# Two transformer blocks on one core: the second block without its dummy TensorE products

## The reference

```python
for layer in range(2):
    mix = hybrid_mixer(x, ...)              # 16 + 12 heads of attention: latent, top-64 of keys, dilated
    z = layer_norm(ALPHA * x + mix, ...)
    x = layer_norm(ALPHA * z + hier_moe(z, ...), ...)

def hier_moe(t, ...):                       # 4 groups of 8 experts, hidden width 256
    lg = t @ rg_w + rg_b                    # one group of four for each token
    le = (t @ re_w + re_b)[chosen group]    # two experts of its eight
    gate = softmax weights of both, times the group's share
    y = sum over experts e of  ((silu(t @ w_gate[e]) * (t @ w_up[e])) * gate[e]) @ w_down[e]
```

## Time and profile before

| what | value |
|---|---|
| median of three runs | 1687.85 us |
| profiled execution | 1691.36 us |
| its span, first to last instruction | 1689.6 us |
| TensorE busy | 1661.9 us, 98% |
| VectorE, ScalarE busy | 858.1, 652.7 us |
| mean granted TensorE clock | 0.993 |
| read from memory | 394.10 MB |

### The profile page before, as it was taken

How to read it: one execution, slowest core, us unless ns; L and a number is a source line. 1 busy time by engine, 2 the same in 40 slices (tenths; PEclk the granted TensorE clock), 3 DMA queues, 4 the chain that set the end, 5 groups by cost and what they waited for, 6 DMA issues and landing times. The chain is left out here.

```text
span 1689.6 us, 23664 instructions
## 1 busy us (share of the span) xinstructions
PE 1661.9 (98%) x9485; PEld 1262.9 (75%) x9485; DVE 858.1 (51%) x1418; ACT 652.7 (39%) x920; POOL 172.9 (10%) x242
## 2 busy tenths in 40 slices
PE   9999999999999999999999999999999999999996
PEld 7888889999788887999988876444548887544453
DVE  6566564444746656444457855322126885532223
ACT  5456443433445544433344542111115464211111
POOL 2020001111102000111111130000002131000000
PEclk9999999999999999999999999999999999999999
DMA  8544545553654454555366428999995634999995
GB/s 321 186 134 148 174 155 195 180 193 109 240 179 145 150 175 150 196 178 196 102 222 190 151 90 316 409 424 423 424 386 173 185 101 148 334 425 422 423 423 214
DMA packets 156285, 396.64 MB, mean 235 GB/s; under 512 B 20496, under 2 KB 85008, under 8 KB 135696
## 3 DMA queue, kind: packets, MB, share of 16 engines
q1 hardware_dynamic: 156176, 395.18, 64.3%
HBM read 394.10 MB, written 1.05 MB: 234 GB/s over the span
## 5 line engine op out<-in xcount | busy, mean ns | idle before, releaser
L918 PE MATMUL ps<-split,split 128*128 128x256 f32 (+3 forms) x1872 | 631.3, 337 | 1.2 <-DVE split L911 0.7
L922 PE MATMUL ps<-split,split 128*128 128x256 f32 (+3 forms) x1872 | 627.7, 335 | 0.2
L919 PE MATMUL ps<-split,split 128*128 128x256 f32 (+3 forms) x1872 | 623.5, 333 | 0.0
L896 DVE TENSOR_TENSOR split<-ring,split 128x2048 fp32r<-128x2048 f32 x136 | 312.6, 2305 | 253.9 <-ACT split L889 253.8
L918 PEld LDWEIGHTS ps<-split,split 128*128 128x128 f32 x1872 | 351.5, 188 | 36.7 <-issue 2.1
L922 PEld LDWEIGHTS ps<-split,split 128*128 128x128 f32 x1872 | 351.7, 188 | 35.9 <-DVE split L2293 1.3
L919 PEld LDWEIGHTS ps<-split,split 128*128 128x128 f32 x1872 | 352.9, 188 | 33.0 <-issue 0.5
L889 ACT ACTIVATE split<-ring 128x2048 fp32r<-128x2048 f32 x136 | 260.3, 1915 | 278.0 <-PE ps L922 268.9
L1775 PE MATMUL ps<-ring,arena 128*64 128x512 f32 x512 | 112.8, 592 | 0.0
L2943 DVE SCALAR_TENSOR_TENSOR arena<-arena,ps 128x256 f32<-128x256 f32 x32 | 15.4, 481 | 167.1 <-ACT arena L2218 131.6
L1775 PE MATMUL ps<-arena 128*64 128x512 f32 x256 | 98.8, 592 | 0.0
(11 more groups left out here) (262 smaller groups left out, 1781.9 us busy)
## 6 DMA issues: line engine op xcount, KB each, us to landing
ring<-in_w_in SPq DMA_DIRECT2D x52, 1024.0 KB, 5.1
ring<-in_w_gate_up SPq DMA_DIRECT2D x44, 1024.0 KB, 5.3
ring<-in_expert_w_down SPq DMA_DIRECT2D x32, 1024.0 KB, 11.6
ring<-in_expert_w_gate SPq DMA_DIRECT2D x24, 1024.0 KB, 11.5
ring<-in_expert_w_up SPq DMA_DIRECT2D x24, 1024.0 KB, 13.5
ring<-in_w_down SPq DMA_DIRECT2D x22, 1024.0 KB, 4.9
ring<-in_w_in SPq DMA_DIRECT2D x28, 768.0 KB, 4.6
high<-in_expert_w_down SPq DMA_DIRECT2D x16, 1024.0 KB, 11.5
```

The costliest lines, as they stand in the source:

```text
L896: nc.vector.tensor_tensor(split(slot), slot, split(high[:, n % HIGH, :]), ALU.subtract).then_inc(low_done.sem, 1)
L918: nc.tensor.matmul(acc, sh, mh, start=start, stop=False)
L919: nc.tensor.matmul(acc, *second, start=False, stop=False)
L922: return nc.tensor.matmul(acc, *third, start=False, stop=stop)
```

## The change

The calls of `keep_running` in the loop of the second block are taken out, all six. In one execution with one pass in each layer these are 32 dummy products in each layer (16 ahead of `turn_z`; 8 and 4 behind the router, with a wait between them; 4 ahead of the gathers), 22 behind the experts of the first layer, and 5 between the two halves of the second layer's `turn_stream`: 91 in all. The waits stay where they are. The calls in the first block and the 26 products at the start of the second stay too.

```diff
--- before.py
+++ after.py
@@ -1484,8 +1484,6 @@
                         mm = nc.tensor.transpose(acc[:, half * SEQ + t * P:half * SEQ + (t + 1) * P], a, ident[:])
                         if t == TT - 1 and half == 1:
                             fill(mm, ("xT", b))
-                    if t == 0 and l > 0:
-                        keep_running(bank2(("A", 1)), 5)
 
             def turn_z(l):
 
@@ -1694,7 +1692,6 @@
                 pair_out(7, l)
                 output_unit(2, l, js=(1,))
                 output_unit(3, l)
-                keep_running(bank2(("xT2", 3)), 16)
                 turn_z(l)
                 acc = bank2(("router", 0))
                 for n, k in enumerate((0, 2, 1, 3, 4, 6, 5, 7)):
@@ -1705,9 +1702,7 @@
                                               start=(n == 0 and t == 0), stop=(n == KT - 1 and t == TT - 1))
                 fill(mm, ("router", 0))
 
-                keep_running(bank2(("ranks", 0)), 8)
                 pe.wait_ge(hot_done.sem, hot_done.at(l, 1))
-                keep_running(bank2(("ranks", 0)), 4)
                 pe.wait_ge(chosen_done.sem, chosen_done.at(l, 1))
                 acc = bank2(("ranks", 0))
                 of_tile = chosen_flat.rearrange("p (t n) -> p t n", t=TT)
@@ -1820,7 +1815,6 @@
 
                     first = pass_ == 0
                     if first:
-                        keep_running(bank2(("sc", 0, 3)), 4)
                         pe.wait_ge(split_low.sem, split_low.at(l, TT))
                     else:
                         wait_apart(pe, sc_added.sem, sc_added.at(lp - 1, 4))
@@ -1882,8 +1876,6 @@
 
                     with pe.If(passes <= done):
                         skip_pass(PASSES - done)
-                        if l < LAYERS - 1:
-                            keep_running(bank2(("yg", 0, 0, 0)), 22)
                     with pe.Else():
                         moe_pass(done)
                         if done + 1 < PASSES:
```

## The result

The change made the kernel slower: 1699.43 us as the median of five runs (1696.51 to 1702.97), against 1686.42 us before (five runs, 1686.04 to 1688.36). The ratio is 1.0066 with a 95% interval of 1.0055 to 1.0077, so +9 to +13 us with +11.1 in the middle; the medians alone differ by 13.0. The forecast was 1706 us, its range 1693 to 1715. The profiled execution took 1696.51 us, its span 1694.7 us.

The account below looks back on a forecast made before the run. It took TensorE's granted clock as decisive, with late expert starts not given back. Two layers of 3.1 - 0.8 + 4.9 make 14.4, plus 3.5 between layers: +17.9 us on the 1687.85 median, 1706 us, range 1693 to 1715.

Parts of the forecast that it names:

- A: 16 dummies out ahead of the turns: clock falls 3.56 us earlier, turns and router slow, +3.1 us a layer.
- B: 12 dummies out ahead of the ranks: start 1.7 us sooner, products at half clock +0.9; -0.8 us a layer.
- C: 4 dummies out ahead of the gathers: gathers and some gate and up products at half clock, +4.9 us a layer.
- early return: Rival: the gathers themselves bring the clock back, C only 2.6 us; 1700 us in all; chance 0.17.
- D: 27 dummies out between the layers: clock falls in 7.3 idle us, second turns and projection slow, +3.5 us once.
- Only columns slow: Rival: half clock costs a product its columns only, gathers start each 0.160 us; 1693 us; chance 0.06.
- Late return: Rival: gate and up products do not restore the clock, only the second gathers do; C 12.4, 1721 us; chance 0.07.
- faster: Rival: clock falls and returns as before, only the rank dummies' delay goes, -3.5 us; 1684.4 us; chance 0.04.

Follow-up runs that it names:

- e10: Kernel before with each second-block dummy of 512 columns replaced by one f32 product of 36 columns, the router's form: 1702.75 us against 1686.99, ratio 1.0100.
- b1: The kernel before, unchanged, profiled once more: 1688.2 us in one run.
- e7: Kernel before without the dummies ahead of turns, ranks and gathers; the 22 and 5 between the layers stay: 1699.77 us, ratio 1.0067.
- e9: Changed kernel with four dummies added in each layer's router, one behind every fourth product: 1699.68 us, ratio 1.0062 to the kernel before.
- e2: Kernel before without only the 16 dummies ahead of the turns in each layer: 1691.22 us, ratio 1.0025.
- e4: Kernel before without only the 22 dummies behind the experts and the 5 between the turns: 1688.46 us, ratio 1.0002.
- a1: The changed kernel, all six calls out, run once more for another profile: 1698.88 us, ratio 1.0061 to the kernel before.
- e3: Kernel before without only the 4 dummies ahead of the gathers in each layer: 1690.10 us, ratio 1.0015.

## Why the prediction was right, and which steps were not

The mechanism was right: what the dummies do for the second block is to keep the clock or to bring it back, and without them the same products run at half of it. e10 is the proof that idleness as such is not the cause: there TensorE never stops in these layers, and the clock is lost. Over the 93 runs of the changed kernel, b1 and the experiments (mean clock and span of each, half-clock time as twice what the clock lacks of 1 times the span) the time grows by 0.30 us for each microsecond at half clock, with a correlation of 0.95. The slope is rough, since the mean clock is given to 0.001, which is 3.4 us at half clock; and time at half clock in which TensorE waits or issues dummies off the path costs nothing. The size, +18 us, was about half as much again as the +11 to +13 measured. Step by step:

- **A, the turns.** Forecast +3.1 us a layer, by letting the fall come earlier by as much as the dummies had lasted. In four layers of the changed kernel it fell in the router as before twice (8.9 and 8.8 us after the last projection product, before 8.7), and about 3 us after it twice, once coming back in the turns and once not. The last router product starts 9.6, 10.6, 9.6 and 13.7 us after the last projection product, against 9.7 before: +1.2 us in the mean. The prediction took one course for the only one; e7 and e9 show it in their first layers. Measured alone (e2) both layers together are +4.2 us.
- **B, the ranks.** Forecast -1.7 and +0.9. In the profile the ranks start 3.6 us after the router's last product instead of 5.3, and take 3.59 instead of 2.72 us up to the gathers: -1.7 and +0.9. Exact, against this profile of before and no other, as the last step says.
- **C, the gathers.** Forecast +4.9. Gathers to gate product took 6.80 and 6.91 us against 4.08: +2.7 and +2.8. This is the rival "early return" (2.6): the clock comes back while gathers run and before any gate product, 5.6 to 5.9 us after they begin in the four layers of the changed kernel. The argument that 192 columns leave the array too little to do was wrong.
- **D, between the layers.** Forecast +3.5, measured +0.5 in the profile and nothing that can be told in e4 and e7. The clock did fall in the idle time. But I counted its return from the start of the projection, and it came back 5.3 us after the turns began, 1.5 us into the projection; the prediction's own low bound, 1.8, had counted from there and was still too high. The 1.5 us of projection at half clock left no trace: from its first product to the last output projection product the layer took 148.4 us as before (148.5).
- **The base.** The parts were worked out against a profile whose layers took 21.85 us each and added to the median of runs that took less. In those, as in b1, the twelve dummies run wholly or in part at full clock, so B gains nothing. Against b1's undisturbed second layer the changed kernel's first is later by 0.3 us at the last router product, by another 0.2 at the ranks, 1.0 at the gathers and 2.7 at the gate products, 4.3 us in all: there B is a loss of 1.2 us and not a gain of 0.8. That I noted the 3.5 us between this execution and the median, and did not ask what they were, was the oversight; it happened to offset part of the others: against its own base the sum said 1709.3 us, where the profiled executions took 1696.5 and 1699.6. With the steps as measured above the sum is 2 x (1.2 - 0.8 + 2.7) + 0.5 = 6.7 us, against 5.2 and 8.3 between the profiles. So parts some 11 us too dear and a base from which the change looks some 5 us too cheap met in a number 7 us from the result: that 1706 us is as near as it is, is in part luck.

Of the rivals, "early return" came nearest, with 1700 us against 1699.43. Its course of the clock over the gathers is what all four layers show; its number is luck in part as well, since it had A at 3.1 and D at 2.7 and used the same base. "Only columns slow" falls: 27 gathers of 192 columns started in 5.70 us at half clock, 0.21 us each, not 0.16. "Late return" and "faster" did not occur in any of the profiles. Two small sums of the prediction are off, without effect on the forecast: the high end of its spread adds up to 1711.6 us, not 1713, and "only columns slow" to 2.4 us in both layers, not 2.6.

Left open: what decides in one execution whether the clock falls in the idle time ahead of the turns or only in the router. The same kernel did both, in one execution.

## What to carry to other kernels

Fillers for TensorE are judged by the clock and not by idle time: in e10 a filler in the form of the router's products, over which the clock had fallen, was worse than none (1.0100 against 1.0066). Where a filler runs at half clock it stands in the way for nearly twice as long (0.426 us against 0.223), so ask of each one what ends last behind it, at both clocks. And before a sum is made against one profiled execution, its own clock stretches are compared with the mean clock of other runs: here the same kernel, unchanged, had 6.8, 3.4 or 0 us at half clock in a layer, and the layer took 21.85, 20.19 or 19.32 us.

## What the runs showed of the hardware

- 36-column f32 products keep TensorE busy without a gap and lose the clock all the same: e10's first layer was busy for all of its 24.64 us at a mean clock of 0.72. The f32 transposes can bring it back. In the second layer of the changed kernel nothing but transposes ran from 1429.85 to 1432.77 us, where the clock went from 0.50 to 1.00. The Trainium skill says in "TensorE: Matmul & The Clock Gate", section "Part 4: PE-mode transpose", that full clock does not engage for transposes, which do not count as busy in the same way. This trace shows the contrary for f32 transposes of 128 columns. It does not happen each time: in a1's second layer the clock was still at 0.50 after the 3.47 us of the same transposes.
- At half clock the f32 products of 36 and of 192 columns start at one pace here: the 192-column gathers every 0.21 us (27 in 5.70 us) and the router's 36-column ones every 0.214, against 0.11 and 0.115 at full clock. So each loses nearly its whole time again, and not its columns alone.
- Idle time does not bring the clock down at a fixed moment: 3.39 us idle ahead of the turns left it at 1.00 in the first layer of the changed kernel and not in the second; in e3 the clock fell within the 1.27 idle microseconds behind the ranks, which themselves stood behind 0.56 idle ones.
